# Transposes of two steps back issued before the dense matmuls of an attention step, in the three mixers of a two-block transformer kernel

## The reference: what is computed

```python
def block1(x):
    x = x + 0.5 * swiglu(rms_norm(x))
    aq, ak, av, hq, hf, hi, hg = split(rms_norm(x) @ w_in)
    mixed = concat([dilated_attention(aq, ak, av), norm(hgrn2(hq, hf, hi)) * silu(hg)])
    x = x + mixed @ w_out
    return x + 0.5 * swiglu(rms_norm(x))

def layer2(h, l):                       # l = 0, 1
    q, kc, vc, ks, vs, kw, vw, gates, u, bg, cg = split(h @ w_in[l])
    o = g0 * cmp_attention(q, compress(kc), compress(vc)) \
      + g1 * sel_attention(q, ks, vs) + g2 * win_attention(q, kw, vw)
    m = concat([o, short_conv(u, bg, cg)]) @ w_o[l]
    h = layer_norm(ALPHA * h + m)
    return layer_norm(ALPHA * h + (swiglu(h) if l == 0 else moe_swiglu(h)))
```

## Time and profile before

| | us |
|---|---|
| median of 3 runs | 2700.65 |
| lowest, highest | 2699.31, 2701.22 |
| the profiled execution's own time | 2695.72 |
| its span, first to last instruction | 2693.9 |
| busy in the span: PE | 2529.3 |
| DVE | 1366.7 |
| ACT | 1046.8 |

### The profile page before, as it was taken

How to read it: one execution, slowest core, us unless ns; L and a number is a source line. 1 busy time by engine, 2 the same in 40 slices (tenths; PEclk the granted TensorE clock), 3 DMA queues, 4 the chain that set the end, 5 groups by cost and what they waited for, 6 DMA issues and landing times.

```text
span 2693.9 us, 38016 instructions
## 1 busy us (share of the span) xinstructions
PE 2529.3 (94%) x15246; PEld 2025.2 (75%) x15246; DVE 1366.7 (51%) x2011; ACT 1046.8 (39%) x1422; POOL 82.0 (3%) x72
## 2 busy tenths in 40 slices
PE   7999999998999998899989999989987999999993
PEld 6888888776788886776768888677765787888872
DVE  4433435565442444466343323256653666666666
ACT  4222234344321223345342222234543556555552
POOL 1000010001000000000000000000000000000000
PEclk9999999999999999999999999999998899999997
DMA  4222232101232231311113222122103577777773
GB/s 146 101 102 78 108 110 95 55 32 55 94 109 94 94 109 51 106 74 48 63 52 107 107 79 105 67 90 94 48 32 147 202 274 263 274 271 267 270 263 138
DMA packets 50751, 328.29 MB, mean 122 GB/s; under 512 B 5856, under 2 KB 5984, under 8 KB 19168
## 3 DMA queue, kind: packets, MB, share of 16 engines
q1 hardware_dynamic: 45184, 310.60, 32.1%
q0 software_dynamic: 4032, 13.88, 1.4%
q10 hardware_dynamic: 1440, 2.50, 0.3%
HBM read 317.51 MB, written 9.44 MB: 121 GB/s over the span
## 4 chain that ended last, share of the span: by engine, by line
PE 86%; DVE 6%; ACT 4%; DMA 2%; issue 2%; POOL 1%; ACTq 0%; DVEq 0%; SPq 0%; POOLq 0%
PE ps L2264 16%; PE ps L2266 16%; PE ps L2265 16%; PE ps L921 5%; PE ps L1527 3%; PE ps L1513 3%; PE ps L1528 3%; PE ps L1529 3%; PE ps L1570 2%; PE ps L1556 1%; PE ps L426 1%; PE ps L1572 1%; PE ps L1571 1%; PE ps L976 1%; PE ps L1011 1%
## 5 line engine op out<-in xcount | busy, mean ns | idle before, releaser
L2264 PE MATMUL ps<-xh,wh 128*128 128x512 f32 x1344 | 533.8, 397 | 37.6 <-DVE xl L2123 13.3
L2265 PE MATMUL ps<-xl,wh 128*128 128x512 f32 x1344 | 530.6, 395 | 0.0
L2266 PE MATMUL ps<-xh,wl 128*128 128x512 f32 x1344 | 529.8, 394 | 0.0
L1896 DVE TENSOR_TENSOR wl<-raw,wh 128x2048 fp32r<-128x2048 f32 (+3 forms) x137 | 326.2, 2381 | 153.0 <-ACT wh L1891 153.0
L1891 ACT CAST wh<-raw 128x2048 fp32r<-128x2048 f32 (+3 forms) x137 | 270.1, 1972 | 326.8 <-PE ps L2266 291.3
L1745 DVE TENSOR_TENSOR wml<-raw_m,wmh 128x2048 fp32r<-128x2048 f32 (+1 forms) x146 | 307.0, 2115 | 118.3 <-ACT wmh L1605 117.6
L2264 PEld LDWEIGHTS ps<-xh,wh 128*128 128x128 f32 x1344 | 256.8, 191 | 96.6 <-issue 22.7
L1605 ACT CAST wmh<-raw_m 128x2048 fp32r<-128x2048 f32 (+1 forms) x146 | 257.6, 1770 | 106.4 <-PE ps L1513 72.6
L2265 PEld LDWEIGHTS ps<-xl,wh 128*128 128x128 f32 x1344 | 256.7, 191 | 54.4 <-issue 1.0
L2266 PEld LDWEIGHTS ps<-xh,wl 128*128 128x128 f32 x1344 | 256.7, 191 | 54.4
L2266 PE MATMUL ps<-ah,wl 128*128 128x512 f32 x528 | 205.6, 389 | 0.0
(11 more groups left out here) (364 smaller groups left out, 3862.0 us busy)
## 6 DMA issues: line engine op xcount, KB each, us to landing
raw_m<-in_moe SPq DMA_DIRECT2D x104, 1024.0 KB, 5.1
raw<-in_ffn_up SPq DMA_DIRECT2D x65, 1024.0 KB, 4.8
raw_m<-in_moe SPq DMA_DIRECT2D x32, 768.0 KB, 4.2
raw<-in_in SPq DMA_DIRECT2D x20, 1024.0 KB, 4.8
raw<-in_ffn_down SPq DMA_DIRECT2D x12, 1536.0 KB, 6.4
raw<-in_ffn_down SPq DMA_DIRECT2D x12, 1280.0 KB, 5.3
raw<-in_cmp SPq DMA_DIRECT2D x8, 1024.0 KB, 4.8
raw<-in_out SPq DMA_DIRECT2D x8, 1024.0 KB, 4.8
```

Of the source, the lines that this page charges most:

```text
L1896: nc.vector.tensor_tensor(wl[:, slot, 0:size], raw[:, slot, 0:size], wh[:, slot, 0:size].bitcast(F32), ALU.subtract).then_inc(lo_ready, 1)
L2264: nc.tensor.matmul(dst, hi_w, hi_x, start=(k == 0), stop=False)
L2265: nc.tensor.matmul(dst, hi_w, lo_x, start=False, stop=False)
L2266: return nc.tensor.matmul(dst, lo_w, hi_x, start=False, stop=(k == last_k))
```

## The change

In both of PE's loops over the steps, `turn(s-2)` now stands behind `scores(s)` and ahead of the dense matmuls. In the later mixers `turn_cmp` moves with it. The programs of the other engines keep their order, and the semaphores and their counts are the same.

```diff
@@ -552,10 +552,11 @@
             for s in range(STEPS1 + 3):
                 if s < STEPS1:
                     scores(s)
+                if 0 <= s - 2 < STEPS1:
+                    turn(s - 2)
+                if s < STEPS1:
                     for x in range(6 * s, 6 * s + 6):
                         dense_h(x)
-                if 0 <= s - 2 < STEPS1:
-                    turn(s - 2)
                 if s >= STEPS1:
                     dense_a(0, s - STEPS1)
@@ -1024,12 +1025,12 @@
             for s in range(STEPS + 3):
                 if s < STEPS:
                     scores(s)
-                for x in range(s * DENSE, min((s + 1) * DENSE, 240)):
-                    conv(2 + x // 24, x % 24, x % 24 + 1)
                 if 0 <= s - 2 < STEPS:
                     turn(s - 2)
                 if 8 <= s < 12:
                     turn_cmp(s - 8, s - 2)
+                for x in range(s * DENSE, min((s + 1) * DENSE, 240)):
+                    conv(2 + x // 24, x % 24, x % 24 + 1)
                 if s >= 4 and s % 2 == 0:
                     product((s - 4) // 2)
```

## The result

The changed kernel takes 2704.27 us (median of 10 runs, 2702.44 to 2710.19). The kernel before, by then also run 10 times, has a median of 2697.5 us (2694.6 to 2702.7). The ratio is 1.0028, with a 95% interval from 1.0018 to 1.0039, and the medians are 6.8 us apart: it is slower, by 0.3%. (A ratio here is estimated from the runs and differs a little from the quotient of the medians.) Two single runs in this study of over 8000 us, one of the kernel before (8229 us) and one of the changed kernel (8636 us), are left out of every median and ratio.

What follows compares the result with a forecast made beforehand. PE was taken as the bound (86% of the last-ending chain). turn_cmp 5.2 + 5.2 us and the first mixer 0.8 us sum to +11.2 us, on the median 2700.65 giving 2711.9 us; range 2706 to 2719.

Steps and rivals of the forecast that it cites:

- the mechanism and its place: Steps 8 to 11, later mixers: turn_cmp waits for its own step's copy, no longer covered by the dense block; +5.2 us per mixer.
- The rival in which the tail swallows the delay: Steps 24 to 31: PE's delay falls into existing waits for ACT and DVE, leaving 2701 to 2706 us; chance 0.10.
- the time on which the sum was put: Whole kernel: +11.2 us put on the median of the runs, 2700.65 us, giving 2711.9 us.
- the forecast's own lower bound: Whole kernel: 2706.5 us, low end of the forecast's own range to 2715, with turn_cmp at 8.0 us.
- turn_cmp, 10.4 us forecast: Steps 8 to 11, two later mixers: +1.76, +1.22, +1.10, +1.10 us in each, 10.4 us together; bounds 8.0 and 11.2.
- the rival "faster": ACT's copies come early, splits finish earlier, PE's waits in front of scores shrink; 2695.5 us; chance 0.04.
- "turn in the later mixers: nothing": Later mixers: turn ahead of the dense block neither loses nor gains, as its inputs come from earlier iterations; 0 us.
- The view of the chain: Whole kernel: 86% of the last-ending chain is PE, so changing PE's order counts only through its idle time.
- First mixer, 0.8 us forecast: First mixer, step 14: turn waits for copy(11), delaying scores(15); +0.8 us, bounds 0 and 1.5; other steps swallow their losses.
- The rival of the clock: Later mixers, steps 8 to 11: idle gaps halve PE's clock, 2.1 us per dense block; 2716 or 2728 us; chance 0.12.

## Why the prediction was right and wrong

**Right: the mechanism and its place.** `turn_cmp` waits for the copy of its own step, the chain `scores`, `masked`, `exp`, `copy` has lost its cover, and the loss is in steps 8 to 11 of the two later mixers. The eight waits are 11.7 us in all (some 13 were forecast). Taking the cover away in parts gave 11.7, 6.2 and 0 us of wait, and putting `turn_cmp` back removed the loss.

**Right: the early turn in the later mixers waits for nothing, and the tail gives nothing back.** Steps 24 to 29 take the same to 0.01 us in both kernels (3.15, 2.43, 4.71, 2.37, 4.42, 4.30 us), and a difference of 3.25 us in the second mixer enters and leaves them. The rival in which the tail swallows the delay is refuted.

**Wrong: the time on which the sum was put, 3.15 us.** The step reads "the median of the runs is 2700.65, 5 us above that execution, and I put the sum on the median". That was a median of three; ten runs gave 2697.5. The range had 2 us "for the difference between executions", too little for a kernel whose runs scatter by 8 us. On the median of ten the same sum makes 2708.7, and the forecast's own lower bound becomes 2697.5 + 8.0 - 2 = 2703.5, below the 2704.27 measured. So this step alone put the time outside the range. The miss as a whole, 2711.9 - 2704.3 = 7.6 us, is 3.15 us from this base, 2.1 from `turn_cmp`, 2.0 from `turn` in the later mixers and 0.5 from the first mixer, all told below, with 0.1 us over.

**Wrong in size: turn_cmp, 10.4 us forecast, 8.3 measured.** Step by step 1.09, 1.10, 0.98 and 0.98 us in the second mixer, where 1.76, 1.22, 1.10 and 1.10 were forecast. Most of it is step 8. The prediction took the distance of `exp(8)` from `scores(8)` from the trace of before, 2.57 us. It is 2.03 us after (`scores` at 1194.32, the last row of `exp(8)` at 1196.35). ACT after, from step 6 to step 8, and DVE's `masked(8)`:

```profile
1189.13 0.41 ACT L1098 COPY pt<-ps 128x128 f32<-128x128 f32 x2
1189.43 1.05 ACT L1074 CAST wh<-raw 128x1024 fp32r<-128x1024 f32 x1
...
1196.35 0.18 ACT L1089 ACTIVATION_READ_ACCUMULATOR sc<-sc,st 128x1 f32 x1
1196.44 0.41 ACT L1098 COPY pt<-ps 128x128 f32<-128x128 f32 x2
...
1194.98 0.42 DVE L1284 CUSTOM_DVE_ANT_0 sc<-ps,mask 128x256 f32<-128x256 f32 x1
```

and before:

```profile
1190.76 0.43 ACT L1097 COPY pt<-ps 128x128 f32<-128x128 f32 x2 [1.11 <-PE ps L991]
1191.08 1.06 ACT L1073 CAST wh<-raw 128x1024 fp32r<-128x1024 f32 x1
...
1195.71 0.41 DVE L1283 CUSTOM_DVE_ANT_0 sc<-ps,mask 128x256 f32<-128x256 f32 x1
```

Before, the copy of one of these steps waits 1.11 us for PE's late `turn`, and the half split behind it (L1073, the part of the weights that ACT prepares) starts at 1191.08. After, it starts at 1189.43. DVE's split follows it, and so does `masked(8)`, which stands behind a split on DVE: 1194.98 instead of 1195.71. This is the mechanism of the rival "faster", which I had dismissed as a whole because "ACT's order has `exp(s)` first". It can't remove the wait, but it does take 0.57 us off one step in each mixer: `turn_cmp` is 2.51 us behind `scores(8)`, not 3.08. Changing only steps 8 to 11 gave the 3.09 us back, so here this is shown, not argued.

**Wrong: "turn in the later mixers: nothing".** It gains 0.06 us in each of the steps 2 to 7 and 12 to 23, some 2 us in the two mixers, and part of the 0.1 us by which each of the steps 9 to 11 came out below forecast will be the same. The view of the chain has "work that changes place on PE costs the same" in it, and that sentence fails: its neighbours count. In the steps 2 to 7 this is seen only where step 2 begins at the full level of the clock; the third mixer's after, behind a low step 1, takes 0.07 us more for the six.

**First mixer, 0.8 us forecast, 0.3 us in the trace after.** The step that the forecast was made for did as told: `turn` waits 0.55 and 0.18 us, step 14 takes 5.13 us instead of 4.19. What was missed is that steps 3, 4, 8, 10 and 12 lose 0.1 to 0.3 us each as well, and that most of all this is won back elsewhere: step 6 4.42 us instead of 4.89, step 5 2.96 instead of 3.38, steps 9 and 13 3.8 instead of 4.2. PE's waits for DVE fell from 8.0 to 5.7 us. The forecast's place for the fall of the clock, on the other hand, was the later mixers only, and it is here that it comes in four traces of six, for 3.1 us.

With these measured sizes the prediction's sum is 8.3 - 2.0 + 0.3 = 6.6 us against the 6.8 us between the medians. That they agree so closely is partly luck, since the interval of the ratio runs from 4.9 to 10.5 us.

**The rival of the clock** decided nothing in the profiled executions of the changed kernel's later mixers, and was right in kind: the same edit made the clock fall in one of its gaps in one trace, and longer gaps (2.10 us) in both mixers. Over all traces it came behind 2 of the 30 gaps of 1.4 to 1.5 us in front of `turn_cmp`, and behind both of 2.10 us. It costs 1.6 us each time, not 2.1, since the level comes back before the dense block is over or soon behind it: in the rows of step 8 above, the first pair of `scores(9)` takes 0.39 us again. The Trainium skill ("TensorE: Matmul & The Clock Gate", section "A second HAM failure mode: psum-queue depth-cycling") has short idle times between groups of matmuls swing the clock, where they come often enough. The traces agree in that such gaps were sometimes followed by a fall. That they came often was not enough here: four in four steps on end, 16 of 1.4 to 1.5 us in the changed kernel's two traces, were followed by none.

**Left open.** Whether the first mixer costs the changed kernel a fraction of a us or 3: the fall of the clock is in four traces of six, but the medians with and without the change in this mixer differ by 0.1 us on one chip and 1.8 us on another, less than these runs tell apart. What decides, at equal waits, whether the clock falls: the idle time, the transposes that now stand next to it, or the moment at which it comes were not varied one by one. And the 0.45 us between the two later mixers.

## What to carry to other kernels

Before work is moved ahead of a block on an in-order engine, ask of each piece which step's result it needs. What needs only results of earlier steps can go first; what needs a result of its own step must stay behind as much of the block as its chain is long, and the price of too little is the uncovered part (here 0.23 us for each 128x512 matmul; 7 of 10 were enough, 3 were not). If an early producer frees the other engines sooner, the distances read from the trace of before shorten in the steps behind it, so the size of the new wait should be worked out with the earlier times. A base from three runs is uncertain by the whole scatter of the runs, and the range must hold it.

## What the runs showed of the hardware

- TensorE's clock fell to 1.2 GHz behind idle times in the middle of dense work, but not each time: behind gaps of 2.10 us in 2 places of 2, behind gaps of 1.4 to 1.5 us in front of `turn_cmp` in 2 of 30, behind three gaps that sum to 1.5 us within 2.6 us, in steps 10 and 14 of the first mixer, in 4 traces of 6, and behind one of 1.48 us in the first mixer in none of 12. At waits alike to 0.01 us it fell in one execution and stayed in another. Each fall cost 1.5 to 1.6 us.
- From the start of four 128x128 transposes to the start of what follows it was 0.41 us between `scores` and a wide matmul and 0.53 us between a wide matmul and `scores`. By order alone 12 steps take 51.70, 52.41 or 52.66 us.
- PE's waits for the weights of the mixture-of-experts stage changed from trace to trace between 0 and 14.4 us with nothing changed there. That is twice the effect that was measured here.
